# The last norm of a transformer kernel: two of its four tiles are moved from VectorE to ScalarE and GpSimd

## The chip, the cores and the metric

The kernel runs on one core of a Trainium2 chip. The metric is the device time of one execution in microseconds (us); lower is better. The engines are TensorE (PE in the profile; its weight loads are PEld), VectorE (DVE), ScalarE (ACT), GpSimd (POOL) and SyncE (SP), which here only issues transfers.

## The reference

Two transformer blocks run over 512 tokens of width 1024, in float32. The second ends in a mixture of experts. The change lies in the last two steps: the two expert rows of each token are weighted and added to the residual `x`, and the sum is normalised and multiplied by the vector `final_norm`.

```python
def _rmsnorm(x, g):
    x32 = x.astype(jnp.float32)
    y = x32 * lax.rsqrt(jnp.mean(x32 * x32, axis=-1, keepdims=True) + EPS)
    return (y * g.astype(jnp.float32)).astype(x.dtype)

def second_block(...):
    ...
        y = _hierarchical_moe(h2, w_router_group[layer], ..., w_down[layer])
        x = x + y.reshape(B, T, D)
    return _rmsnorm(x, final_norm)
```

## The kernel before, in words

The 512 tokens are four tiles (`MT` = 4) of 128 partitions by 1024 columns, held in `X`. The experts work on 24 steps of gathered rows, and GpSimd stores each step's results to `expert_rows` in HBM with an indirect transfer (`store`, L2431). When the last of these has landed, `last_pool` (L2574) issues eight indirect gathers, two for each tile, in the order of the tiles: `R1` and `R2` are the rows of a token's first and second expert, both in the arena `RING`. Nothing else is on GpSimd's queue behind them.

`last_dve` on VectorE has three kinds of step for a tile m:

- `summed(m)`: it waits for both gathers of the tile and does two `scalar_tensor_tensor` of 128x1024 (L2582, L2585), each X = R * weight + X.
- a reciprocal of one column (L2590), behind ScalarE's square root of the mean square.
- the norm (L2592): one `scalar_tensor_tensor` of 128x1024, Y = X * reciprocal * GP, where `GP[:, 1, :]` holds `final_norm` on all partitions.

Its order, written out by hand, is summed(0), summed(1), normed(0), summed(2), normed(1), summed(3), normed(2), normed(3), and the reciprocal is the first half of `normed`. `last_act` on ScalarE takes each tile as its sum is done: the squares with their sum (L2605, written to a scratch part of `WK`) and the root (L2608). SyncE stores the tiles in order (L2638), 512 KB each, tile m when the shared semaphore `norm_scaled` (`l_y`) has counted m + 1 norms. A `Sig` is a range of counts on a semaphore; `.at(v)` is its v-th count. Other parts of the kernel use the same kinds of instruction: L228 is a ScalarE `Copy` with one scale per partition, L1085 and L2030 are two-input multiplies or adds on GpSimd, L1731 and L1858 are its multiplies by one value per partition, L149 is VectorE's subtraction of 128x2048 with both inputs in SBUF, L2405 is the first indirect transfer of the experts.

Of the kernel before, what the change touches and what calls it, by code (L numbers as in the profile page):

```python
# [9 lines left out]
ALU = mybir.AluOpType  # L10
ACT = mybir.ActivationFunctionType
# [6 lines left out]
MT = T // P  # L18
# [42 lines left out]
def program(nc, a, out):  # L61
# [5 lines left out]
    with ctx:  # L67
        def sb(name, shape, dt=fp32):
            return ctx.enter_context(nc.sbuf_tensor(name, shape, dt))

        def sem(name):
            return ctx.enter_context(nc.semaphore(name))
# [15 lines left out]
        X = sb("X", [P, MT, D])  # L88
        Y = sb("Y", [P, MT, D])
# [11 lines left out]
        GP = sb("GP", [P, 2, D])  # L101
# [9 lines left out]
        stat = sb("stat", [P, 64])  # L111
# [82 lines left out]
        class Norm:  # L194
# [15 lines left out]
            def squares(self, act, m):  # L210
                if self.src_by_tile:
                    act.wait_ge(self.ready[0][m], 16)
                else:
                    act.wait_ge(self.ready[0], self.ready[1](m))
                for i, (c0, c1) in enumerate(self.parts):
                    nc.scalar.activation(SIL[:, 0:2, :].rearrange("p a b -> p (a b)")[:, 0:c1 - c0],
                                         self.src[:, m, c0:c1], ACT.Square,
                                         accum_out=stat[:, 8 * i + m:8 * i + m + 1]).then_inc(self.sq.sem, 1)
                    act.wait_ge(*self.sq.at(m * len(self.parts) + i + 1))
                    nc.scalar.activation(stat[:, 16 + 8 * i + m:17 + 8 * i + m], stat[:, 8 * i + m:8 * i + m + 1],  # L220
                                         ACT.Sqrt, bias=stat[:, 60:61], scale=1.0 / (c1 - c0)).then_inc(self.stats.sem, 1)
# [537 lines left out]
        def wait_gain(eng, r):  # L759
            eng.wait_ge(s_gain[r % 2], 16 * (r // 2 + 1))  # L760
# [1801 lines left out]
        l_st = Sig("norm_stats", MT)  # L2562
        l_r = Sig("norm_rstd", MT)
        l_y = Sig("norm_scaled", MT)
        s_out = sem("out_stored")
        R1, R2 = [RING[:, i * MT * D:(i + 1) * MT * D].rearrange("p (m n) -> p m n", m=MT) for i in range(2)]

        def last_pool(pool):
            for s in range(2):
                pool.wait_ge(m_st[s], 16 * (NSTEP // 2))  # L2570
            pool.wait_ge(m_gu, NSTEP)
            for m in range(MT):
                for k, r in enumerate((R1, R2)):
                    nc.gpsimd.indirect_dma_start(  # L2574
                        r[:, m, :], None, slot_dram[:, :],
                        bass.IndirectOffsetOnAxis(ap=si[:, k, m:m + 1], axis=0)).then_inc(l_g[m], 16)

        def last_dve(dve):
            wait_gain(dve, 5)
            def summed(m):  # L2580
                dve.wait_ge(l_g[m], 16 * 2)
                nc.vector.scalar_tensor_tensor(X[:, m, :], R1[:, m, :], w1_[:, m, :], X[:, m, :], ALU.mult, ALU.add  # L2582
                                               ).then_inc(l_a.sem, 1)
                dve.wait_ge(*l_a.at(2 * m + 1))
                nc.vector.scalar_tensor_tensor(X[:, m, :], R2[:, m, :], w2_[:, m, :], X[:, m, :], ALU.mult, ALU.add  # L2585
                                               ).then_inc(l_a.sem, 1)

            def normed(m):
                dve.wait_ge(*l_st.at(m + 1))
                nc.vector.reciprocal(stat[:, 32 + m:33 + m], stat[:, 16 + m:17 + m]).then_inc(l_r.sem, 1)  # L2590
                dve.wait_ge(*l_r.at(m + 1))
                nc.vector.scalar_tensor_tensor(Y[:, m, :], X[:, m, :], stat[:, 32 + m:33 + m], GP[:, 1, :],  # L2592
                                               ALU.mult, ALU.mult).then_inc(l_y.sem, 1)

            summed(0)
            for m in range(1, MT):
                summed(m)
                normed(m - 1)
            normed(MT - 1)

        def last_act(act):
            nc.scalar.activation(stat[:, 62:63], stat[:, 60:61], ACT.Sqrt)
            for m in range(MT):
                act.wait_ge(*l_a.at(2 * (m + 1)))
                nc.scalar.activation(SIL[:, 0:2, :].rearrange("p a b -> p (a b)"), X[:, m, :], ACT.Square,  # L2605
                                     accum_out=stat[:, m:m + 1]).then_inc(l_sq.sem, 1)
                act.wait_ge(*l_sq.at(m + 1))
                nc.scalar.activation(stat[:, 16 + m:17 + m], stat[:, m:m + 1], ACT.Sqrt, bias=stat[:, 60:61],  # L2608
                                     scale=1.0 / D).then_inc(l_st.sem, 1)

        out_v = out[0].rearrange("(m p) n -> p m n", p=P)
        s_init = sem("init")
# [29 lines left out]
        def _(pool):  # L2642
# [79 lines left out]
                pool.dma_start(h2_dram[m * P:(m + 1) * P, :], Y[:, m, :]).then_inc(s_h2, 16)  # L2722
            moe_pool(pool)
            last_pool(pool)

        @block.scalar
        def _(act):
            act.wait_ge(s_init, 3)
            nc.scalar.activation(stat[:, 62:63], stat[:, 60:61], ACT.Sqrt).then_inc(s_init, 1)
            n1.high(act, 0)  # L2730
            split_to(act, "act", 1)
            n1.high(act, 1)
            n1.squares(act, 0)
            n1.squares(act, 1)
            n1.high(act, 2)
            n1.squares(act, 2)
            n1.high(act, 3)
            n1.squares(act, 3)
            even_act(act)
            d_ev.act(act, n2)  # L2740
            f0.act(act)
            d_f0.act(act, n3)
            odd_act(act)
            nsa_act(act)
            d_od.act(act, n4)
            f1.act(act)
            d_f1.act(act, n5)
            p_2.take(act, "act", {0: forget_split_act, 3: forget_act}, {1: turn_take(0), 2: turn_take(1), 4: turn_take(2), 5: turn_take(3)})
            two_act(act)
            out2_act(act)  # L2750
            router_act(act)
            moe_act(act)
            last_act(act)

        @block.vector
        def _(dve):
# [26 lines left out]
            router_dve(dve)  # L2783
            moe_dve(dve)
            last_dve(dve)

        @block.tensor
# [82 lines left out]
```

## Time and profile before

| | |
|---|---|
| median of three runs | 1869.71 us (1867.91 to 1870.28) |
| the profiled execution, its own time | 1870.54 us |
| its span, first to last instruction | 1868.4 us |
| TensorE, VectorE, ScalarE, GpSimd busy | 94%, 41%, 30%, 13% of the span |
| last instruction of TensorE ends | about 1837 us |
| first sum of the last stage starts | 1848.46 us |
| last norm starts, ends | 1864.04 us, 1865.3 us |

The profile is one execution. The span leaves out 2.1 us of that execution's own time, and the median of the runs lies 0.8 us under it. Busy shares are means over the whole program; the stretch in question is the last 20 us of it, where TensorE does nothing and VectorE, ScalarE, GpSimd and the DMA engines hand tiles to each other.

### The profile page before, as it was taken

Reading aid. Unit: us, or ns where it says so; the run is one execution under the profiler, and the core shown is the slowest. Engines: PE = TensorE matmul, PEld = TensorE weight load, DVE = VectorE, ACT = ScalarE, POOL = GpSimd, SP = SyncE. Lnnn points to the kernel's source line nnn. Section 1 sums busy time; section 2 is a strip of 40 time slices with the busy share of each in tenths; the row PEclk is TensorE's granted clock in tenths of the full one; section 3 lists DMA queues with packets and bytes.
Section 4 is the critical chain, followed back from the end, with each engine's and each line's share of the span. In section 5 each row is a group of like instructions: output and inputs, shape, how many; then the busy total and the mean of one; then the engine's idle time right before and its main releaser. Section 6 shows DMA issues by size and latency. Waiting matters only on the chain. (4 is left out here: it accounts for less than half of the span.)

```text
span 1868.4 us, 21875 instructions
## 1 busy us (share of the span) xinstructions
PE 1761.1 (94%) x9057; PEld 1301.8 (70%) x9057; DVE 759.1 (41%) x1211; ACT 554.8 (30%) x853; POOL 237.9 (13%) x283
## 2 busy tenths in 40 slices
PE   7998999999999999898999999999999978999993
PEld 6778888888878786577888888878766763333331
DVE  5445232233365345735322232263257462333334
ACT  5235322232342124626222222252247310000001
POOL 3000000000002003310000000010014303333322
PEclk9999999999999998999999999999999978999997
DMA  7223333322232218211433323233320166999974
GB/s 236 91 68 86 94 90 99 103 90 91 91 118 92 85 51 247 80 46 47 112 94 108 90 90 105 98 113 91 91 90 24 54 268 255 362 397 395 378 318 148
DMA packets 179490, 260.93 MB, mean 140 GB/s; under 512 B 18888, under 2 KB 134792, under 8 KB 167120
## 3 DMA queue, kind: packets, MB, share of 16 engines
q1 hardware_dynamic: 155824, 204.66, 32.6%
q0 software_dynamic: 19552, 25.75, 4.4%
q10 hardware_dynamic: 4032, 29.36, 4.0%
q8 instruction: 60, 0.98, 0.2%
q14 instruction: 22, 0.18, 0.0%
HBM read 297.50 MB, written 29.40 MB: 175 GB/s over the span
## 5 line engine op out<-in xcount | busy, mean ns | idle before, releaser
L149 DVE TENSOR_TENSOR RING_R<-RING,RING_R 128x2048 fp32r<-128x2048 f32 (+1 forms) x110 | 250.1, 2276 | 617.2 <-ACT RING_R L146 617.1
L168 PE MATMUL PB<-RING_R,OPS_R 128*128 128x512 f32 (+1 forms) x1056 | 415.3, 393 | 14.1 <-DVE RING_R L149 7.1
L170 PE MATMUL PB<-RING_R,OPS_R 128*128 128x512 f32 (+1 forms) x1056 | 409.3, 388 | 0.0
L169 PE MATMUL PB<-RING_R,OPS_R 128*128 128x512 f32 (+1 forms) x1056 | 409.2, 388 | 0.0
L146 ACT ACTIVATE RING_R<-RING 128x2048 fp32r<-128x2048 f32 (+1 forms) x110 | 208.3, 1897 | 309.9 <-DMA RING<-in_ffn_w_down 137.3
L168 PE MATMUL PB<-OPS_R,RING_R 128*128 128x512 f32 (+1 forms) x768 | 286.3, 373 | 1.2 <-DVE OPS_R L275 1.2
L170 PE MATMUL PB<-OPS_R,RING_R 128*128 128x512 f32 (+1 forms) x768 | 285.9, 372 | 0.0
L169 PE MATMUL PB<-OPS_R,RING_R 128*128 128x512 f32 (+1 forms) x768 | 285.8, 372 | 0.0
L168 PEld LDWEIGHTS PB<-RING_R,OPS_R 128*128 128x128 f32 x1056 | 199.0, 188 | 58.8 <-DVE RING_R L149 9.1
L170 PEld LDWEIGHTS PB<-RING_R,OPS_R 128*128 128x128 f32 x1056 | 199.0, 188 | 40.9
L169 PEld LDWEIGHTS PB<-RING_R,OPS_R 128*128 128x128 f32 x1056 | 199.3, 189 | 38.8 <-issue 0.2
L168 PEld LDWEIGHTS PB<-OPS_R,RING_R 128*128 128x128 f32 x768 | 145.4, 189 | 26.9 <-DVE OPS_R L275 1.6
L169 PEld LDWEIGHTS PB<-OPS_R,RING_R 128*128 128x128 f32 x768 | 145.4, 189 | 24.8
L170 PEld LDWEIGHTS PB<-OPS_R,RING_R 128*128 128x128 f32 x768 | 145.4, 189 | 24.9
L731 ACT ACTIVATE WK<-PB 128x512 f32<-128x512 f32 x44 | 26.4, 599 | 273.0 <-PE PB L170 272.9
L2510 ACT ACTIVATE WK<-PB 128x256 f32<-128x256 f32 x24 | 9.2, 383 | 285.8 <-PE PB L2469 285.8
L2537 DVE TENSOR_TENSOR WK<-PB,WK 128x256 f32<-128x256 f32 x24 | 14.7, 614 | 157.5 <-ACT WK L2510 157.5
L366 ACT ACTIVATE Z<-PB,stat 128x512 f32<-128x512 f32 (+1 forms) x34 | 23.0, 676 | 132.7 <-PE PB L170 132.7
L2685 POOL DMA_DIRECT2D GP<-in_od_cmp_v_w x1 | 1.2, 1171 | 468.7 <-DVE X L542 468.7
L2469 PE MATMUL PB<-RING,WK 128*64 128x512 f32 x256 | 58.6, 612 | 0.0
L2469 PE MATMUL PB<-Z,WK 128*64 128x512 f32 x256 | 56.7, 595 | 0.0
L2469 PE MATMUL PB<-OPS,WK 128*64 128x512 f32 x256 | 56.7, 595 | 0.0
(356 smaller groups left out, 1857.2 us busy)
## 6 DMA issues: line engine op xcount, KB each, us to landing
RING<-in_ffn_w_gate SPq DMA_DIRECT2D x44, 512.0 KB, 4.0
RING<-in_ffn_w_up SPq DMA_DIRECT2D x44, 512.0 KB, 5.3
RING<-in_ffn_w_down SPq DMA_DIRECT2D x44, 512.0 KB, 3.9
RING<-in_w_expert_gate SPq DMA_DIRECT2D x16, 1024.0 KB, 8.2
RING<-in_w_expert_up SPq DMA_DIRECT2D x16, 1024.0 KB, 11.6
OPS<-in_w_expert_gate SPq DMA_DIRECT2D x16, 1024.0 KB, 11.6
OPS<-in_w_expert_up SPq DMA_DIRECT2D x16, 1024.0 KB, 13.7
Y<-in_w_expert_down ACTq DMA_DIRECT2D x14, 1024.0 KB, 10.0
```

The source lines that it names most:

```text
L146: nc.scalar.activation(RING_R[:, high], RING[:, raw], ACT.Copy).then_inc(s_whi, 1)
L149: nc.vector.tensor_tensor(RING_R[:, raw], RING[:, raw], RING_R[:, high].bitcast(fp32), ALU.subtract).then_inc(s_wlo, 1)
L168: nc.tensor.matmul(o, x[0], w[0], start=start, stop=False)
L169: nc.tensor.matmul(o, x[0], w[1], start=False, stop=False)
L170: return nc.tensor.matmul(o, x[1], w[0], start=False, stop=stop)
L366: t = nc.scalar.activation(dst, src, func, scale=rstd) if self.norm.deferred else nc.scalar.activation(dst, src, func)
L731: nc.scalar.activation(SIL[:, k, :], PB[:, BANK[k], :], ACT.Silu).then_inc(self.sl.sem, 1)
L2469: t = nc.tensor.matmul(PB[h, 2 + s % 2, :], XgT[:, s % 2, k, h], moe_gu[g][:, b, :, k, :], start=(k == 0), stop=(k == KT - 1))
L2510: nc.scalar.activation(Hs[:, s % 2, :], PB[:, 2 + s % 2, 0:DE], ACT.Silu).then_inc(m_si, 1)
L2537: nc.vector.tensor_tensor(Hh[:, s % 2, :].rearrange("q (j p) -> q p j", j=2), f(PB[:, 2 + s % 2, DE:2 * DE]), f(Hs[:, s % 2, :]), ALU.mult ...
L2685: pool.dma_start(cmp_w1[1], w1_v[1]).then_inc(s_w1, 16)
```

## The change

Tiles 0 and 1 are normalised by two engines: ScalarE multiplies X in place by the reciprocal (`scaled`, a `Copy` with a scale per partition), and GpSimd multiplies the result by `GP` into Y (`last_rows_pool`). ScalarE's order becomes squares(0), squares(1), scaled(0), squares(2), scaled(1), squares(3). VectorE keeps all four reciprocals and the norms of tiles 2 and 3; the norm of tile 2 stands behind summed(3) and, so that the counts of `l_y` keep the order of the tiles, waits for GpSimd's second multiply. The waits of SyncE's stores are unchanged.

```diff
+        l_xs = Sig("down_scaled", 2)
...
-            def normed(m):
+            def root_inverse(m):
                 dve.wait_ge(*l_st.at(m + 1))
                 nc.vector.reciprocal(stat[:, 32 + m:33 + m], stat[:, 16 + m:17 + m]).then_inc(l_r.sem, 1)
+
+            def normed(m):
                 dve.wait_ge(*l_r.at(m + 1))
+                if m == 2:
+                    dve.wait_ge(*l_y.at(2))
                 nc.vector.scalar_tensor_tensor(Y[:, m, :], X[:, m, :], stat[:, 32 + m:33 + m], GP[:, 1, :],
                                                ALU.mult, ALU.mult).then_inc(l_y.sem, 1)
 
             summed(0)
-            for m in range(1, MT):
-                summed(m)
-                normed(m - 1)
-            normed(MT - 1)
+            summed(1)
+            root_inverse(0)
+            summed(2)
+            root_inverse(1)
+            summed(3)
+            root_inverse(2)
+            normed(2)
+            root_inverse(3)
+            normed(3)
+
+        def last_rows_pool(pool, m):
+            pool.wait_ge(*l_xs.at(m + 1))
+            nc.gpsimd.tensor_tensor(Y[:, m, :], X[:, m, :], GP[:, 1, :], ALU.mult).then_inc(l_y.sem, 1)
...
+            def scaled(m):
+                act.wait_ge(*l_r.at(m + 1))
+                nc.scalar.activation(X[:, m, :], X[:, m, :], ACT.Copy, scale=stat[:, 32 + m:33 + m]).then_inc(l_xs.sem, 1)
+
+            squares(0)
+            squares(1)
+            scaled(0)
+            squares(2)
+            scaled(1)
+            squares(3)
...
             last_pool(pool)
+            wait_gain(pool, 5)
+            last_rows_pool(pool, 0)
+            last_rows_pool(pool, 1)
```

## Rows read from the trace of the kernel before

**Rows 1.** The page, part 1: busy time and share of the span.
```profile
PE 1761.1 (94%) x9057; PEld 1301.8 (70%) x9057; DVE 759.1 (41%) x1211; ACT 554.8 (30%) x853; POOL 237.9 (13%) x283
```
**Rows 2.** The chain that ended last, its end: start us, length us, what.
```profile
1845.67 6.18 DMA RING<-expert_rows,slot_i
...
1854.48 0.08 DVE stat L2590
...
1854.59 1.28 DVE Y L2592
1855.87 1.21 DVE X L2582
...
1861.01 1.29 DVE X L2585
...
1862.33 1.16 ACT WK L2605 x2
...
1863.84 0.17 DVE stat L2590
...
1864.04 1.28 DVE Y L2592
```
**Rows 3.** Timeline, 1850 to 1866 us: start, us, engine, line; in brackets the idle before.
```profile
1850.86 1.02 POOL L2574 DMA_INDIRECT RING<-expert_rows,slot_i  x1 [0.30 <-issue]
...
1853.19 1.28 DVE L2585 SCALAR_TENSOR_TENSOR X<-RING,Z,X 128x1024 f32<-128x1024 f32 x1
...
1854.51 1.06 ACT L2605 ACTIVATE WK<-X 128x1024 f32<-128x1024 f32 x1 [1.93 <-DVE X L2585]
...
1855.69 0.29 ACT L2608 ACTIVATE stat<-stat 128x1 f32<-128x1 f32 x1
...
1855.90 9.79 SPq L2638 DMA_DIRECT2D out_x<-Y  x4
```
**Rows 4.** DMA issues, us to landing: 1848 to 1849, 1850.5 to 1852, stores.
```profile
RING<-expert_rows,slot_i POOLq DMA_INDIRECT x1, 6.2
...
RING<-expert_rows,slot_i POOLq DMA_INDIRECT x2, 6.1
...
out_x<-Y SPq DMA_DIRECT2D x4, 512.0 KB, 2.7
```
**Rows 5.** Groups by line and form, whole span: busy us, mean ns, idle before.
```profile
L228 ACT ACTIVATE Y<-X,stat 128x1024 f32<-128x1024 f32 x8 | 9.1, 1142 | 0.9 <-DVE stat L254 0.9
...
L1085 POOL TENSOR_TENSOR Z<-Z,gam 128x2048 f32<-128x2048 f32 x2 | 11.2, 5588 | 61.0 <-DVE Z L1075 61.0
...
L1858 POOL TENSOR_SCALAR ST<-ST,two_den,ones 128x512 f32<-128x512 f32 x8 | 8.3, 1035 | 5.4 <-DVE two_den L1997 4.7
...
L2030 POOL TENSOR_TENSOR WK<-WK 128x512 f32<-128x512 f32 x6 | 7.6, 1274 | 4.1 <-ACT WK L1941 4.1
```
**Rows 6.** Timelines of GpSimd and VectorE, 1246 to 1252 and 581 to 583.
```profile
1246.17 0.44 POOL L1731 TENSOR_SCALAR Y<-ident,stat,ones 128x128 f32<-128x128 f32 x1
...
1247.03 2.59 POOL L1731 TENSOR_SCALAR Y<-ident,stat,ones 128x128 f32<-128x128 f32 x1
1247.10 2.29 DVE L149 TENSOR_TENSOR RING_R<-RING,RING_R 128x2048 fp32r<-128x2048 f32 x1 [1.65 <-ACT RING_R L146]
...
1249.61 2.47 POOL L1731 TENSOR_SCALAR Y<-ident,stat,ones 128x128 f32<-128x128 f32 x1
1249.31 2.46 DVE L149 TENSOR_TENSOR RING_R<-RING,RING_R 128x2048 fp32r<-128x2048 f32 x1
...
581.71 2.28 DVE L149 TENSOR_TENSOR RING_R<-RING,RING_R 128x2048 fp32r<-128x2048 f32 x1
581.88 5.58 POOL L1085 TENSOR_TENSOR Z<-Z,gam 128x2048 f32<-128x2048 f32 x1 [45.89 <-DVE Z L1075]
```
**Rows 7.** GpSimd's first indirect transfer, and L1085 by source.
```profile
1546.82 1.08 POOL L2405 DMA_INDIRECT Z<-h_rows,idx_i  x1 [27.35 <-DVE idx_i L2314]
...
L1085 POOLq MODIFY_POOL_CONFIG  x2: 37/37/37, 536.0 to 536.0; - x2
```

More of the change, by code:

```diff
@@ L2595, in last_dve, with squares @@
             summed(0)
-            for m in range(1, MT):
-                summed(m)
-                normed(m - 1)
-            normed(MT - 1)
+            summed(1)
[10 more added lines that the diff above has]
+            nc.gpsimd.tensor_tensor(Y[:, m, :], X[:, m, :], GP[:, 1, :], ALU.mult).then_inc(l_y.sem, 1)
         def last_act(act):
             nc.scalar.activation(stat[:, 62:63], stat[:, 60:61], ACT.Sqrt)
-            for m in range(MT):
+            def squares(m):
                 act.wait_ge(*l_a.at(2 * (m + 1)))
```

## The prediction

> **What bounds the kernel.** TensorE is busy for 94% of the span [rows 1], but it has ended about 30 us before the program does (the table above). So I went straight to the chain that ended last. From 1851.87 to the end it is VectorE with one gap: sums, reciprocals and norms stand back to back, 1.2 to 1.3 us each, and only after the last sum (ends 1862.30) does the chain go over to ScalarE for squares and root, and come back for the last reciprocal and norm [rows 2]. That wait, 1862.30 to 1863.84, is not idle even now: the norm of tile 2 stands in it, beside the chain and for nothing. What stands ahead of the last sum sets the end, and that is, besides the sums, the norms of tiles 0 and 1, 1.28 us each. The view of the DMA issues says when the sums could start at the earliest. The second gather of tile 2 is issued at about 1848.15 and lands 6.2 us later, near 1854.35; that of tile 3 is issued at 1850.86 and lands 6.1 us later, near 1856.95 [rows 3, 4]. VectorE reaches those tiles at 1855.87 and, one half before 1861.01, at 1859.7, so there is slack of 1.5 and 2.8 us before the gathers bind. After the last norm come one store, 2.7 us to landing [rows 4], and 0.4 us to the end of the span.
>
> **What the change takes off VectorE.** Two norms ahead of the last sum go. summed(2) then starts after summed(1) and a reciprocal, at 1854.56 instead of 1855.87 (its gathers landed 0.2 us earlier), ends at 1857.15, and with the next reciprocal (0.09 us) summed(3) can start at 1857.24, its gathers just landed. Undisturbed it would end at 1859.83, 2.5 us before now.
>
> **What it puts elsewhere.** ScalarE finishes the root of tile 1 at 1855.98 [rows 3]. scaled(0) is a Copy with a scale per partition; the same form takes 1.14 us at L228, where it stands between roots and squares with no table load beside it [rows 5], so I charge none. It ends at 1857.15. squares(2) with its root runs 1857.18 to 1858.65 (1.47 us, as 1854.51 to 1855.98 in [rows 3]), scaled(1) to 1859.80, in time for squares(3). ScalarE is no bound.
>
> GpSimd's multiply of 128x1024 with two SBUF inputs is in no row. 128x512 takes 1.27 us (L2030) [rows 5]. Below: the second 512 columns at the rate of its one-input multiply, (1035 - 440)/384 = 1.55 ns each (L1858 and the first row of [rows 6]), give 2.07 us. Above: the rate of L1085, 5588/2048 = 2.73 ns a column [rows 5], gives 2.79 us. I take 2.3 us: 1.27 us less a fixed quarter microsecond (0.44 us for 128 columns less 128 at 1.55 ns), twice, plus the quarter once. The Trainium skill (GPSIMD Engine Reference, Performance versus the Vector engine) gives 4497 ns for 2048 columns; a line through that and the 1.27 us would make 2.35 us, an estimate that changes nothing in the sum.
>
> **The wait that the change makes.** GpSimd would get tile 0 at about 1857.2, the moment when summed(3) starts, and both engines' instructions read two SBUF operands. The trace of before shows what happens. L1731 on GpSimd takes 0.44 us alone; the one issued at 1247.03, just before VectorE's L149 (1247.10 to 1249.39), takes 2.59 us and ends 0.23 us after L149. The L149 behind it, recorded from 1249.31, takes 2.46 us for 2.29: it lost 0.17 us while GpSimd's 0.44 us instruction was served. The next L1731, issued after that, again took as long as L149 ran: 2.47 us [rows 6]. L1085 fits as well: issued 0.17 us into an L149, it takes 5.58 us, of which 2.11 lie under L149. So they take turns, whole instructions at a time. The Trainium skill says so outright (SBUF — State Buffer, Who interferes with whom): a VectorE instruction with two SBUF inputs and a GpSimd instruction that reads SBUF use one read port, under an exclusive lock, held for the instruction. By that rule, the rows agree; it speaks against this change, since the sums and the norms are of that kind. With turns the end is the one summed below; without them it is the first rival's, 1.8 us earlier.
>
> In [rows 6] VectorE got the port when GpSimd's instruction was issued 0.07 us ahead of it, so I give it the first turn:
>
> - summed(3), first half: 1857.24 to 1858.52. GpSimd's multiply of tile 0 waits under it.
> - GpSimd has the port from 1858.52. 0.2 us of its 2.3 are already spent while waiting (0.23 us after L149's end for an instruction of 0.44), so it ends at 1860.6; VectorE gets in 0.14 us before that (1249.48, from 0.17 us lost, against 1249.62).
> - summed(3), second half: 1860.46 to 1861.75, against 1862.30 now. Of the 2.5 us gain 0.55 is left.
> - GpSimd's second multiply (tile 1 is scaled by 1859.80) is issued at 1860.6, waits under that half, and runs to 1861.75 + 2.1 = 1863.85.
> - squares(3) and root end at 1863.25, no longer the last to come: normed(2) waits for GpSimd's second multiply, to 1863.9, although tile 2's root has been there since 1858.65.
> - normed(2) 1863.9 to 1865.2, reciprocal 3 behind it, normed(3) 1865.3 to 1866.6. Before it ended at 1865.32: 1.3 us later.
>
> So the new wait `l_y.at(2)` costs twice: the norm of tile 2 is pushed out of the wait for the last squares, and 1.28 us of it lie between GpSimd and the last norm. Behind the waiting norm stand the last reciprocal and norm, and behind those SyncE's stores 2 and 3. The stores themselves: tile 0's goes at 1860.6 instead of 1855.9, tile 1's at 1863.9, then 1865.2 and 1866.6. Before, the last two norms ended 1.6 us apart, at 1863.7 and 1865.3, and every store still landed in 2.7 us [rows 4]; at 1.3 to 1.4 us apart a store waits at worst 0.3 us for the one ahead, and I charge nothing. GpSimd has nothing behind its multiplies. On ScalarE squares(3) stands behind scaled(1), ready before it.
>
> Sum: span 1868.4 + 1.3 = 1869.7, own time 1870.54 + 1.3 = 1871.8; from the median, 1869.71 + 1.3 = **1871.0 us**. Each 0.1 us on GpSimd's 2.3 counts twice: 2.07 gives +0.8, 2.79 gives +2.3.
>
> **Rivals.**
>
> *No turns at the port (the change does what it says).* For it: the rows show the port contested by TENSOR_TENSOR, never by SCALAR_TENSOR_TENSOR, which the sums are. Then summed(3) ends at 1859.83, GpSimd's multiplies at 1859.5 and, from 1859.8, at 1862.1; normed(2) to 1863.45, reciprocal 3, normed(3) to 1864.85: 0.5 us earlier, 1869.2 us, or 0.75 earlier with 2.07 us a multiply. Even then GpSimd and not the squares releases normed(2). The full 2.5 us is out of reach, since tile 1 is scaled only at 1859.8. Against: both kinds read two tensors in SBUF. Chance 0.18.
>
> *GpSimd gets the first turn.* Tile 0 is ready 0.04 us before summed(3). Then the first half of summed(3) waits to 1859.36 and ends at 1860.64, the second multiply takes the port to 1862.75, the second half ends at 1863.9, squares and root at 1865.4, norm 3 at 1866.9: 1.6 us later, 1871.3 us. Chance 0.14.
>
> *Slower by more than the measurement can tell.* 0.2% (3.7 us) is about what the runs can tell from no change. One mechanism reaches it: the multiply does not shrink with its columns, or its first use costs extra. If it took L1085's whole 5.59 us [rows 5] each time, the end would be 2 x 3.29 = 6.6 us later again, at 1877.6 us; it decides from 3.5 us a multiply, or from 2.4 us extra once. Against: 2.79 us is the dearest rate, and GpSimd's first indirect transfer took 1.08 us for some 1.0 of the others [rows 7]. The Trainium skill (GPSIMD Engine Reference, Instruction dispatch) has about 6 us for the first call to a freshly loaded kernel; the trace has MODIFY_POOL_CONFIG twice, at L1085, both at 536.0, 46 us before that multiply, so nothing there shows the price. Chance 0.06.
>
> **How the numbers follow.** My forecast 0.60, GpSimd first 0.14, no turns 0.18, much slower 0.06, anything else 0.02. The likeliest alone, +0.8 to +2.3, is 1870.5 to 1872.0. The scatter of three runs is 2.4 us, their median perhaps 0.7. The range takes in the no-turns case less that scatter (1869.0 - 0.7 = 1868.3) and the dearest multiply plus it (1872.0 + 1.2 = 1873.2), and leaves out the 0.06. Every case but that one is within 0.2%: faster 0.02, same 0.91, slower 0.07.
>
> **What would show it.** In the timeline after: one half of summed(3) at 3 us or more, or a GpSimd multiply at 3.4 us or more, in place of 1.28 and 2.3; the chain passing through GpSimd's second multiply into normed(2); normed(3) starting at 1865.3. If no half of summed(3) is above 1.35 us and each multiply is near 2.3, the turns are refuted. A GpSimd instruction above 3.5 us with no VectorE work beside it, or a table load on ScalarE, would make the prediction wrong.

## The result, and the profile after

The changed kernel takes 1875.16 us in the median of 11 runs, against 1869.85 us for the kernel before in its 11. The ratio is 1.0021, 95% interval 1.0013 to 1.0029: 3.9 us longer (2.4 to 5.4), where 1.3 us were forecast. The two medians lie 5.3 us apart, at the upper end of that interval. One of the 11 runs of the changed kernel took 2579 us at a granted clock of 0.65; the ratio leaves it out. The profiled execution has a span of 1874.6 us, against 1868.4.

6.2 us between two profiles is more than the change. Work ahead of the last stage is the same code, and yet the start of the last store of expert rows (L2431), the last event before that stage, stands at 1839.03 before and 1840.61 after, and between 1836.3 and 1841.9 in the profiles of the experiments below. So I count from that start and call what lies between it and the end of the span **the tail**: 1868.4 - 1839.03 = 29.4 us before, 1874.6 - 1840.61 = 34.0 us after, 4.6 us more, which the interval of the ratio holds.

The chain that ended last, of the changed kernel (start us, length us, what), answers to [rows 2]:

```profile
1856.11 1.16 ACT WK L2619 x2
...
1857.59 1.05 ACT X L2627
...
1858.78 3.35 POOL Y L2613
1862.13 3.29 POOLq L67
...
1865.52 1.29 DVE Y L2597
1866.81 0.08 DVE stat L2591
1866.89 0.03 issue
1866.91 1.29 DVE Y L2597
```

The chain now leaves VectorE at the sum of tile 1, goes through ScalarE's scaling to GpSimd, and comes back only for norms 2 and 3. (The piece of 3.29 us is GpSimd's second multiply; this view names it by the instruction of line 67 that was recorded over it.) The timeline of the changed kernel shows the turns (columns as in [rows 3]):

```profile
1840.61 0.97 POOL L2431 DMA_INDIRECT expert_rows<-ST,slot_rows  x1 [3.75 <-DVE ST L2545]
...
1857.39 1.28 DVE L2586 SCALAR_TENSOR_TENSOR X<-RING,Z,X 128x1024 f32<-128x1024 f32 x1
1857.50 1.13 ACT L2627 ACTIVATE X<-X,stat 128x1024 f32<-128x1024 f32 x1
...
1858.66 1.27 DVE L2583 SCALAR_TENSOR_TENSOR X<-RING,Z,X 128x1024 f32<-128x1024 f32 x1
...
1858.78 6.64 POOL L2613 TENSOR_TENSOR Y<-X,GP 128x1024 f32<-128x1024 f32 x2 [4.93 <-ACT X L2627]
...
1859.96 3.25 DVE L2586 SCALAR_TENSOR_TENSOR X<-RING,Z,X 128x1024 f32<-128x1024 f32 x1
...
1865.52 1.29 DVE L2597 SCALAR_TENSOR_TENSOR Y<-X,stat,GP 128x1024 f32<-128x1024 f32 x1 [2.23 <-POOL Y L2613]
...
1866.91 1.29 DVE L2597 SCALAR_TENSOR_TENSOR Y<-X,stat,GP 128x1024 f32<-128x1024 f32 x1
```

GpSimd's first multiply is recorded from 1858.78 and ends at 1862.13; the second ends at 1865.42. Neither is a multiply of 3.3 us: the first waits under the first half of summed(3) until 1859.93 and then takes 2.2 us, and the second half of summed(3), 3.25 us instead of 1.28, waits under it. The second multiply waits under that half until 1863.21 and takes 2.2 us again. In the tail's own time the last norm ends at 1868.20 - 1840.61 = 27.6 us, before at 1865.32 - 1839.03 = 26.3: 1.3 us later. That is the forecast, and it leaves 3.3 of the 4.6 us unexplained.

Those stand behind the last norm, where the chain and the timeline show nothing. What does show them is the closing barrier of the program, line 67: each engine has a drain there, an instruction that ends only after the work in front of it, and the program ends when all have signalled. First the changed kernel, from 1860 us (count: durations in ns min/median/max, first and last start):

```profile
L67 POOLq EVENT_SEMAPHORE  x2: 17/17/17, 1874.4 to 1874.5; - x2
L67 POOLq DRAIN  x1: 13067/13067/13067, 1861.3 to 1861.3; - x1
L67 ACTq DRAIN  x1: 324/324/324, 1864.4 to 1864.4; - x1
L67 DVEq DRAIN  x1: 1326/1326/1326, 1866.9 to 1866.9; - x1
L67 SPq COMPARE_BRANCH  x1: 38/38/38, 1870.9 to 1870.9; - x1
```

and the same view of the kernel before, from 1855 us:

```profile
L67 POOLq EVENT_SEMAPHORE  x2: 17/17/17, 1868.2 to 1868.3; - x2
L67 POOLq DRAIN  x1: 16502/16502/16502, 1844.9 to 1844.9; - x1
...
L67 SPq COMPARE_BRANCH  x1: 38/38/38, 1868.0 to 1868.0; - x1
```

A drain is recorded from a time when the work in front of it is still running, so I count from the end of that work. Before, GpSimd's drain ran to 1844.9 + 16.5 = 1861.4, 9.5 us behind the end of the last gather's issue (1851.88), and it cost nothing, since SyncE passed its wait for the stores only at 1868.0. After, it runs to 1861.3 + 13.07 = 1874.4, 8.9 us behind the second multiply; the stores were all there at 1870.9, and the program waited 3.4 us more for this drain alone.

### The profile page after: what moved, and what is told of

Same layout as the page of the kernel before. It is cut to its first block and busy times, and to the rows that moved or that the text cites. A ratio compares the mean times of both kernels' runs of the same rounds, so it can differ in the third digit from the quotient of the medians.

```text
span 1874.6 us, 21879 instructions
## 1 busy us (share of the span) xinstructions
PE 1759.2 (94%) x9057; PEld 1300.3 (69%) x9057; DVE 758.1 (40%) x1209; ACT 557.3 (30%) x855; POOL 244.8 (13%) x285
## 3 DMA queue, kind: packets, MB, share of 16 engines
q1 hardware_dynamic: 155824, 204.66, 32.6%
## 5 line engine op out<-in xcount | busy, mean ns | idle before, releaser
L169 PEld LDWEIGHTS PB<-OPS_R,RING_R 128*128 128x128 f32 x768 | 144.7, 188 | 24.8
```

The source lines that it names most:

```text
L169: nc.tensor.matmul(o, x[0], w[1], start=False, stop=False)
```

## The experiments

All times are in us, of one profile each, counted from the start of the last store of expert rows; "last norm" is the end of VectorE's last instruction. Ratios are against runs of the kernel before on the same chip; most of their intervals overlap, so the tails of the profiles carry the argument and the ratios only agree with it.

| kernel | last norm | closing drain ends | tail | ratio (95%) |
|---|---|---|---|---|
| before | 26.3 | 22.3 | 29.4 | |
| after | 27.6 | 33.7 | 34.0 | 1.0021 (1.0013 to 1.0029) |
| after, barrier without GpSimd's drain | 27.4 | none | 30.6 | 1.0007 (0.9998 to 1.0016) |
| before, barrier without GpSimd's drain | 26.2 | none | 29.3 | 0.9996 (0.9987 to 1.0006) |
| before, late one-column memset | 26.5 | 32.5 | 32.8 | 1.0014 (1.0005 to 1.0023) |
| after, no wait in front of norm 2 | 27.3 | 33.7 | 34.0 | 1.0016 (1.0006 to 1.0026) |
| after, memsets for multiplies | 24.4 | 30.5 | 30.8 | 1.0001 (0.9990 to 1.0013) |
| the same, barrier without the drain | 24.7 | none | 27.9 | 0.9993 (0.9982 to 1.0003) |
| before, norms behind all sums | 26.0 | 22.2 | 29.1 | 0.9995 (0.9984 to 1.0005) |
| late memset behind a drain of its own | 26.3 | 23.5 | 29.4 | 1.0001 (0.9989 to 1.0012) |
| after, drains inside the experts | 27.6 | 25.9 | 30.7 | 1.0010 (1.0000 to 1.0019) |
| late memset, one drain ahead of the experts | 26.6 | 32.3 | 32.6 | 1.0017 (1.0006 to 1.0028) |
| tile 0 alone on GpSimd, early | 26.2 | 27.6 | 29.3 | 1.0018 (1.0000 to 1.0036) |
| norms behind the sums, last tile in halves | 26.2 | 22.3 | 29.2 | 1.0002 (0.9993 to 1.0011) |

### Is it the drain? Without it, after and before

```diff
-        block = ctx.enter_context(nc.Block())
+        block = ctx.enter_context(nc.Block(no_gpsimd_drain=True))
```

The changed kernel:

> The changed kernel whose closing barrier leaves out GpSimd's drain. I measure the tail: from the start of the last store of expert rows (L2431) to the end of the span, 29.4 us before, 34.0 us after. Theory (GpSimd's end): its closing drain takes about 9 us behind its last multiply and ends the program; without it the tail is 30.7 us, last norm plus its store, 1.3 above before, and the median comes 3.3 us under the changed kernel. Rival (the end is held by something else that came with the new instructions, such as the one packet more on the instruction queue or the late stores): the tail stays at 34.0.

The kernel before:

> The kernel before, its closing barrier without GpSimd's drain. GpSimd's end: the drain ended at 1861.4 there, 6.9 us before the program did, hidden under the sums and norms, so nothing moves: tail 29.3 us, within 0.1, median within 0.1%. Rival (the barrier form is itself faster or slower): the tail moves by 1 us or more here too, and the gain of the first run is not the drain's.

The changed kernel's tail falls to 30.6 us, its ratio to 1.0007; the kernel before stays at 29.3. The barrier of line 67 in the changed kernel, now without a POOLq DRAIN:

```profile
L67 POOLq EVENT_SEMAPHORE  x2: 17/17/17, 1869.3 to 1869.4; - x2
...
L67 SPq COMPARE_BRANCH  x1: 38/38/38, 1869.1 to 1869.1; - x1
```

GpSimd's semaphore follows SyncE's wait by 0.2 us (1869.1 to 1869.3), where it stood 3.5 us behind it (1870.9 to 1874.4). The barrier's form costs nothing by itself. 3.3 of the 4.6 us are the drain's.

### A late instruction on GpSimd, with no contention

```diff
+        s_late = sem("late_memset")
...
             last_pool(pool)
+            pool.wait_ge(*l_a.at(2 * MT))
+            nc.gpsimd.memset(stat[:, 63:64], 0.0).then_inc(s_late, 1)
```

> The kernel before plus one GpSimd memset of one column (0.1 us) that waits for the last sum (1862.3 in the profile of before), with nothing behind it but the drain. GpSimd's end: the drain then ends 8.9 to 9.5 us after 1862.5, near 1871.7, against 1868.4: tail 32.5 to 33.1 us, with VectorE's times unchanged to 0.1 us. Rival (turns at the port alone make the change slow): a memset reads nothing and blocks nobody, the tail stays at 29.4.

Timeline and closing barrier of this kernel:

```profile
1864.09 1.28 DVE L2586 SCALAR_TENSOR_TENSOR X<-RING,Z,X 128x1024 f32<-128x1024 f32 x1
...
1865.44 0.10 POOL L2727 MEMSET stat<- 128x1 f32 x1 [10.38 <-DVE X L2586]
...
L67 POOLq EVENT_SEMAPHORE  x2: 17/17/17, 1874.5 to 1874.6; - x2
L67 POOLq DRAIN  x1: 9030/9030/9030, 1865.4 to 1865.4; - x1
```

One column set to zero, 0.10 us of work that holds nobody up, makes the tail 3.4 us longer, as the drain behind it takes 9.0 us: 32.8 us, inside the 32.5 to 33.1 expected. What counts is when GpSimd's last work ends, not how much it is.

### The wait that the prediction blamed

```diff
-        l_y = Sig("norm_scaled", MT)
+        l_y = Sig("norm_scaled", 2)
+        l_yp = sem("norm_pool_rows")
...
-                if m == 2:
-                    dve.wait_ge(*l_y.at(2))
...
-            nc.gpsimd.tensor_tensor(...).then_inc(l_y.sem, 1)
+            nc.gpsimd.tensor_tensor(...).then_inc(l_yp, 1)
...
-                sp.wait_ge(*l_y.at(m + 1))
+                sp.wait_ge(*((l_yp, m + 1) if m < 2 else l_y.at(m - 1)))
```

> The changed kernel with a semaphore of its own for GpSimd's two rows, so that the norm of tile 2 no longer waits for them. Norm 2 then runs under the squares of tile 3 and the last norm starts about 2 us earlier (24.3 us after the last store of expert rows instead of 26.3). GpSimd's end: the tail stays at 34.0 all the same. Rival (my prediction's reading, that the wait in front of norm 2 sets the end): the tail falls to 32.0 or below.

The tail stays at 34.0, as expected if the drain sets the end. What I expected of the norms was wrong: the last one starts at 26.0 us, not 24.3. Norm 2 is free to go and runs into GpSimd's second multiply instead:

```profile
1859.39 3.25 DVE L2587 SCALAR_TENSOR_TENSOR X<-RING,Z,X 128x1024 f32<-128x1024 f32 x1
...
1862.75 3.18 DVE L2596 SCALAR_TENSOR_TENSOR Y<-X,stat,GP 128x1024 f32<-128x1024 f32 x1
...
1866.04 1.28 DVE L2596 SCALAR_TENSOR_TENSOR Y<-X,stat,GP 128x1024 f32<-128x1024 f32 x1
```

3.18 us for a norm of 1.28. The wait on a semaphore was only the visible form of the wait for the port; with it gone, 0.3 of its 2.2 us came back.

### Port or any GpSimd work?

```diff
-            nc.gpsimd.tensor_tensor(Y[:, m, :], X[:, m, :], GP[:, 1, :], ALU.mult).then_inc(l_y.sem, 1)
+            nc.gpsimd.memset(Y[:, m, :], 1.0).then_inc(l_y.sem, 1)
```

> The changed kernel with each of GpSimd's two multiplies replaced by a memset of the same 128x1024 of Y: it leaves out the multiplication by the norm's vector for tiles 0 and 1, so GpSimd writes and reads nothing. Theory (turns at a read port): both halves of summed(3) take 1.28 us and the last norm ends at about 23.8 us after the last store of expert rows (27.6 in the changed kernel, 26.3 before). GpSimd's memsets end near 21.8, and its closing drain sets the tail at 31.0 us (34.0 in the changed kernel). Rival (any GpSimd work holds VectorE up): a half of summed(3) stays above 1.6 us and the last norm ends after 26.

(The memset writes all of Y's 1024 columns and reads nothing; that is what "writes and reads nothing" means.) And with the barrier without the drain:

> The same with the closing barrier that leaves out GpSimd's drain (it too leaves out the multiplication by the norm's vector for tiles 0 and 1). If port and drain are the whole loss, this is what moving two norms off VectorE was worth: last norm ended at 23.8 us, tail 26.9 us, 2.5 under the kernel before. If something else keeps the end, the tail stays near 29 or above.

Timeline of the first of the two:

```profile
1859.00 0.95 POOL L2613 MEMSET Y<- 128x1024 f32 x1 [5.08 <-ACT X L2627]
1859.02 1.26 DVE L2583 SCALAR_TENSOR_TENSOR X<-RING,Z,X 128x1024 f32<-128x1024 f32 x1
...
1860.32 1.28 DVE L2586 SCALAR_TENSOR_TENSOR X<-RING,Z,X 128x1024 f32<-128x1024 f32 x1
...
1861.63 0.95 POOL L2613 MEMSET Y<- 128x1024 f32 x1 [1.69 <-ACT X L2627]
...
1862.69 1.28 DVE L2597 SCALAR_TENSOR_TENSOR Y<-X,stat,GP 128x1024 f32<-128x1024 f32 x1 [1.01 <-POOL Y L2613]
```

GpSimd's instruction is issued 0.02 us ahead of VectorE's and writes as many columns as the multiply did, and the two halves of summed(3) take 1.26 and 1.28 us. So it is GpSimd's reading that takes turns with an instruction of two SBUF inputs. This is the rule of the Trainium skill (SBUF — State Buffer, Who interferes with whom), which excepts a GpSimd instruction that only writes; the run agrees. The last norm ended at 24.4, later than the 23.8 I had worked out: norm 2 still waits 1.01 us for GpSimd, whose second row cannot start before ScalarE has scaled tile 1, behind the squares of tile 2. In the run without the drain the gathers landed 0.3 us later, and the tail was 27.9 for 26.9 expected. Free of port and drain, and with a memset of 0.95 us for a multiply of 2.2, two norms fewer on VectorE are worth 1.5 us of tail here, not 2.5. The drain costs 30.8 - 27.9 = 2.9 us in this pair, although the second kernel's gathers landed later.

### The order of VectorE's work alone

```diff
-            summed(0)
-            for m in range(1, MT):
-                summed(m)
-                normed(m - 1)
-            normed(MT - 1)
+            for m in range(MT):
+                summed(m)
+            for m in range(MT):
+                normed(m)
```

> The kernel before with VectorE's order alone changed: the four sums first, then the four norms. VectorE is then never idle behind the last sum. Expected: last norm ends 0.2 to 0.4 us earlier, tail 29.0 to 29.2 us, the median the same within 0.1%. If the norms ahead of the last sum were what set the end as I wrote, the last squares should start 3.9 us earlier and still buy almost nothing, because VectorE's own work is then the bound. Rival: the stores, now 1.3 us apart, queue up and give the gain back, tail 29.4 or more.

29.1 us, as expected. VectorE's timeline goes from the last sum through four norms without idle time:

```profile
1855.82 1.28 DVE L2585 SCALAR_TENSOR_TENSOR X<-RING,Z,X 128x1024 f32<-128x1024 f32 x1
...
1857.22 1.28 DVE L2592 SCALAR_TENSOR_TENSOR Y<-X,stat,GP 128x1024 f32<-128x1024 f32 x1
...
1861.40 1.28 DVE L2592 SCALAR_TENSOR_TENSOR Y<-X,stat,GP 128x1024 f32<-128x1024 f32 x1
```

So the kernel before was within 0.3 us of what VectorE's own twelve instructions allow. What the norms ahead of the last sum cost is VectorE time, not their place.

### What are the 9 us?

A drain of its own behind the gathers, ahead of the late memset:

```diff
+        s_late = sem("late_memset")
...
             last_pool(pool)
+            nc.gpsimd.drain()
+            pool.wait_ge(*l_a.at(2 * MT))
+            nc.gpsimd.memset(stat[:, 63:64], 0.0).then_inc(s_late, 1)
```

> The kernel before with a drain on GpSimd right behind the gathers, then the one-column memset that waits for the last sum, then the closing drain as ever. It asks what the 9 us are. If they are paid once for the indirect transfers issued so far, the second drain is short and the tail is 29.4 us. If every drain at that place costs them, whatever has been issued since the last one, the tail is 32.8 us as with the late memset alone.

```profile
L2726 POOLq DRAIN  x1: 16575/16575/16575, 1843.6 to 1843.6; - x1
...
1861.15 0.10 POOL L2728 MEMSET stat<- 128x1 f32 x1 [10.43 <-DVE X L2586]
...
L67 POOLq DRAIN  x1: 188/188/188, 1861.1 to 1861.1; - x1
```

The first drain takes what the closing one did, in GpSimd's idle time, and the closing one 0.19 us. So the price is paid once, for something that came before the first drain. Nor is it a wait for the gathers to land: in the changed kernel the last of them had landed near 1858.8 (1852.83 + 6.0), 6.6 us before the second multiply ended. In all five kernels with 154 transfers and a late last instruction on GpSimd (the changed kernel, the late memset, no wait, memsets for multiplies, tile 0 alone) the drain ended 8.9 us behind that instruction, whatever it was. To see for what, I moved drains forward. In the changed kernel, one ahead of the experts and one behind every third step's store:

```diff
                 store(s)
+                if s % 3 == 2 and s < NSTEP - 1:
+                    nc.gpsimd.drain()
...
+            nc.gpsimd.drain()
             moe_pool(pool)
```

> The changed kernel with drains on GpSimd where it idles: one ahead of the experts' first gather and one behind the store of every third expert step but the last. The closing drain then has 13 GpSimd transfers behind it instead of 154. If its 9 us grow with the transfers issued since the last drain (9.0 / 154 = 0.058 us each), it takes 0.9 us, ends near 25.8 us and is hidden: tail 30.7 us, last norm at 27.6 as in the changed kernel. If 9 us are due as soon as anything was issued since, the tail stays at 34.0.

and in the kernel before with the late memset, only the one ahead of the experts:

> The kernel before with the late one-column memset and one drain on GpSimd ahead of the experts' first gather, so that 104 transfers lie between it and the closing drain (154 without it). Growing with the transfers: 0.2 + 104 x 0.057 = 6.1 us, ending at 29.7, tail 29.9 us. A fixed price: tail 32.8 as with the memset alone. If only the eight last gathers count: also 32.8.

The drains of the two kernels, the closing ones first with 13 transfers issued since the last drain, then with 104. The rows of transfers are of the view of the DMA issues (us to landing):

```profile
L2451 POOLq DRAIN  x7: 6722/10713/12026, 1603.7 to 1814.2; - x7
...
1814.45 0.98 POOL L2431 DMA_INDIRECT expert_rows<-ST,slot_rows  x1 [9.66 <-DVE ST L2547]
...
expert_rows<-ST,slot_rows POOLq DMA_INDIRECT x1, 6.0
...
L67 POOLq DRAIN  x1: 5289/5289/5289, 1862.4 to 1862.4; - x1
```

```profile
1517.90 0.53 POOL L2723 DMA_DIRECT2D h_rows<-Y  x1 [6.21 <-DVE Y L245]
...
h_rows<-Y POOLq DMA_DIRECT2D x1, 512.0 KB, 9.0
...
L2724 POOLq DRAIN  x1: 10207/10207/10207, 1517.9 to 1517.9; - x1
...
L2728 POOL MEMSET stat<- x1: 99/99/99, 1860.3 to 1860.3; 128x1 f32 x1
...
L67 POOLq DRAIN  x1: 8694/8694/8694, 1860.3 to 1860.3; - x1
```

With 13 transfers the drain ends 1.1 us behind the second multiply (1862.4 + 5.3 = 1867.6, the multiply at 1866.5), is hidden, and the tail is 30.7 us: what the kernel without the drain has. The price does grow with what was issued since the last drain, but not as I had it: 104 transfers cost 8.6 us behind the memset, where 6.1 was expected, and 154 cost 8.9.

The drains further forward show another side. The seven among the experts (11 to 20 transfers each) took 6.7 to 12.0 us, and these were waits for landings: each stands right behind a store, and it ended 0.5 us behind the landing of that store (the first of them 0.9 us). The last one is in the lines above: the store lands at 1814.45 + 6.0 = 1820.5, the drain ends at 1814.2 + 6.7 = 1820.9. The one ahead of the experts, with 50 transfers, ended 1.2 us behind the landing of the last of them (1517.90 + 9.0 = 1526.9, 1517.9 + 10.2 = 1528.1). So a drain waits for transfers that are still on their way, and besides has a price of its own, which the late closing drains show bare. What law that price follows between 13 and 104 transfers, and what GpSimd does in it, stays open: a drain that waits for a landing may hide it.

### Tile 0 alone, early enough for the drain to be hidden

GpSimd gets tile 0 only; its reciprocal stands between the halves of summed(1), norms 1 to 3 behind the last sum.

```diff
-                if m == 2:
-                    dve.wait_ge(*l_y.at(2))
+                if m == 1:
+                    dve.wait_ge(*l_y.at(1))
...
             summed(0)
-            summed(1)
-            root_inverse(0)
+            summed(1, lambda: root_inverse(0))
             summed(2)
...
+            normed(1)
             normed(2)
...
             squares(0)
+            scaled(0)
             squares(1)
-            scaled(0)
             squares(2)
-            scaled(1)
             squares(3)
...
-            last_rows_pool(pool, 1)
```

> Tile 0 alone goes to ScalarE and GpSimd, and early: its reciprocal stands between the two halves of summed(1), ScalarE scales it before the squares of tile 1; VectorE keeps norms 1, 2 and 3, all behind the last sum. GpSimd's multiply ends at about 19 us after the last store of expert rows, its drain at 28, so the end is VectorE's. Turns at the port: the second half of summed(2) takes 3.2 us, last norm ends at 26.8, tail 29.9 us, 0.5 above before, although a norm less is on VectorE. Without turns the last norm would end at 24.9 and the tail be 28.0.

The drain ended at 27.6 and was hidden, and the second half of summed(2) took its turn as expected:

```profile
1854.47 3.32 POOL L2615 TENSOR_TENSOR Y<-X,GP 128x1024 f32<-128x1024 f32 x1 [2.28 <-ACT X L2629]
...
1855.62 3.24 DVE L2588 SCALAR_TENSOR_TENSOR X<-RING,Z,X 128x1024 f32<-128x1024 f32 x1
```

The tail is 29.3, that of the kernel before, and not the 29.9 I had summed (my sum set the last norm 0.6 us too late). VectorE gives a norm of 1.28 us away and loses 1.96 to the turn. What pays the difference was not taken apart; the order alone was worth 0.3 us in the run above. The ratio of 1.0018 has an interval from 1.0000 to 1.0036, too wide to say more than the profile does.

### Trying to beat both

```diff
+            for c in (slice(0, D // 2), slice(D // 2, D)):
+                nc.vector.scalar_tensor_tensor(Y[:, m, c], X[:, m, c], ..., GP[:, 1, c], ...)
...
+            for i, c in enumerate((slice(0, D // 2), slice(D // 2, D))):
+                sp.wait_ge(*l_y.at(MT + i))
+                sp.dma_start(out_v[:, MT - 1, c], Y[:, MT - 1, c]).then_inc(s_out, 16)
```

> No GpSimd: the kernel before with the four sums first, then the norms, and the last tile's norm and store in two halves of 512 columns. Expected: last norm ends at about 26.1 us (25.96 with the order alone, plus the second instruction's fixed cost), the last store is half as large, so tail 28.4 to 28.7 us, 0.7 to 1.0 under before. Rival: a store of rows of 2 KB moves slower or the two queue up, tail 29.0 or more. The median moves by less than the runs can tell either way.

29.2 us: the rival. The two issues of the last tile, by the view of the DMA issues:

```profile
out_x<-Y SPq DMA_DIRECT2D x2, 256.0 KB, 2.5
```

Half the bytes, and 2.5 us to landing in the median instead of 2.7. The best of these orders, the norms behind the sums in whole tiles, has 0.3 us less tail than the kernel before and a ratio that does not tell it from 1.

## Why the prediction was right and where it was wrong

- **The gain on VectorE.** summed(3) started right behind summed(2) and a reciprocal, and its gathers did not hold it up. Right. But "what stands ahead of the last sum sets the end" was too narrow: with both norms moved behind the last sum the tail fell by 0.3 us only, as VectorE's own twelve instructions then set the end.
- **ScalarE.** Copy 1.13 us for 1.14, no table load, no bound. Right.
- **GpSimd's multiply.** 2.2 us once it has the port, where 2.1 of 2.3 were reckoned to be left. Right. With the 0.2 us that the prediction reckoned as spent while waiting that is 2.4 us, near the 2.35 us that the prediction estimated with the 4497 ns for 2048 columns of the Trainium skill (GPSIMD Engine Reference, Performance versus the Vector engine). The upper bound of 2.79 us came from a poor row: the 5.58 us of L1085 hold 2.11 us of waiting, as the prediction itself reads them, so they give no rate.
- **The turns at the port.** VectorE had the first turn though GpSimd's row was ready about when summed(3) began, the second half took 3.25 us, the chain came through GpSimd's second multiply, the last norm ended 1.30 us later than before against 1.3 forecast. Right, and shown three ways: by the multiply, by the memset in its place, and by norm 2 running into the port when its semaphore wait was taken away.
- **The end of GpSimd's queue.** This step failed. I wrote: "GpSimd has nothing behind its multiplies", and in the description of the kernel that nothing else is on its queue behind the gathers. Behind them stands the closing drain, and the sum had no term for it. The forecast took the 3.1 us from the last norm to the end of the span as they were before and added them to the new last norm, 27.6 + 3.1 = 30.7, which is what the kernel without the drain shows. With it the end is GpSimd's last work plus 8.9 us: 24.8 + 8.9 + 0.2 = 33.9, where 34.0 were measured.
- **The rival on the slower side** had the right sign and the right size (0.2%), on the wrong mechanism: neither a dearer multiply nor a first use. No extra first-use cost was seen; both multiplies took 2.2 us with the port.
- It could have been suspected before. The end of the kernel's own drain at 1861.4 stood in the instructions of line 67, 9.5 us behind GpSimd's last work and 7.0 us ahead of the end of the span. If such a drain follows later work too, GpSimd work that ends after about 1868.2 - 9.5 = 1858.7 pushes the end out, and the prediction had the second multiply end at 1863.85: 1863.85 + 9.5 + 0.2 = 1873.6, 5.2 us more, where 4.6 were measured. That trace alone could not say whether the 9.5 us were tied to the gathers just issued; the experiments could.

## What to carry to other kernels

Work given to an engine that was finished moves that engine's end, and the end has a price of its own: look at what closes each queue (here a drain on GpSimd, 9 us behind its last work when 154 of its transfers had gone before, 0.2 us when it had just been drained), not only at the last compute instruction. If GpSimd must work late, drain it earlier in its idle time, or leave the drain out of the barrier where every one of its transfers is waited for otherwise.

A multiply offloaded to GpSimd beside VectorE instructions of two SBUF inputs is no offload: here it took 2.0 us from VectorE to spare it 1.28.

## What the runs showed of the hardware that was not expected

GpSimd's closing drain ended 8.9 us behind its last work with 154 transfers issued and landed (9.3 to 9.5 with the last ones just issued), 8.6 with 104 since the last drain, 1.1 with 13, and took 0.19 us in all with none. Drains right behind a store ended 0.5 us (once 0.9) behind its landing. VectorE's closing drain is recorded with 1.3 us and ScalarE's with 0.3 in the same kernels. A store of half the columns landed only 0.2 us sooner.
